# Last product with the mixed tokens stationary, gate and last norm on rows, plain transposes in place of products with a diagonal

## The reference, cut to what matters

```python
def second_block(x, c, ada_w, ada_b, norm_g, w_in, ..., w_out, final_g):
    mod = silu(c) @ ada_w + ada_b                 # 3 x 1024 numbers, one row for all tokens
    shift, scale, gate = split(mod, 3)
    h = rmsnorm(x, norm_g) * (1 + scale) + shift
    p = h @ w_in
    ...                                           # conv branch, RWKV branch
    m = sigmoid(g_conv) * y_conv + sigmoid(g_rwkv) * y_rwkv
    out = m @ w_out                               # the last product, 1024 x 1024
    x = x + gate * out
    return rmsnorm(x, final_g)
# the first block ends: x = x + swiglu(rmsnorm(x, norm_ffn)); x = rmsnorm(x, norm_final)
```

## Time and profile before

| | before |
|---|---|
| median of 3 runs | 1160.0 us (1159.91 to 1161.25) |
| the profiled execution's own time | 1160.27 us |
| its span | 1158.4 us |
| PE busy | 1142.2 us, 99% |
| DVE busy | 483.4 us, 42% |
| ACT busy | 235.6 us, 20% |
| DMA | 161.03 MB, mean 139 GB/s |

### The profile page before, as it was taken

How to read it: one execution, slowest core, us unless ns; L and a number is a source line. 1 busy time by engine, 2 the same in 40 slices (tenths; PEclk the granted TensorE clock), 3 DMA queues, 4 the chain that set the end, 5 groups by cost and what they waited for, 6 DMA issues and landing times.

```text
span 1158.4 us, 20043 instructions
## 1 busy us (share of the span) xinstructions
PE 1142.2 (99%) x8492; PEld 954.2 (82%) x8492; DVE 483.4 (42%) x1248; ACT 235.6 (20%) x617; POOL 80.8 (7%) x119
## 2 busy tenths in 40 slices
PE   9999999999999999999999999999999999999997
PEld 7888888888888587677776878888888888887886
DVE  4252332525332111011011566656667767666332
ACT  3031221203200110001001522313232231324001
POOL 1100000000033100000000021020202202010000
PEclk9999999999999999999999999999999999999999
DMA  8566555540557336443554233223232322151330
GB/s 297 202 238 237 167 204 183 188 162 19 182 147 238 123 130 203 165 152 121 194 203 165 68 97 93 92 93 103 85 107 92 111 74 74 38 219 38 109 109 37
DMA packets 52650, 161.03 MB, mean 139 GB/s; under 512 B 6449, under 2 KB 12497, under 8 KB 52562
## 3 DMA queue, kind: packets, MB, share of 16 engines
q1 hardware_dynamic: 51554, 158.12, 40.3%
q10 hardware_dynamic: 1008, 1.63, 0.4%
HBM read 158.63 MB, written 1.10 MB: 138 GB/s over the span
## 4 chain that ended last, share of the span: by engine, by line
PE 93%; DVE 6%; DMA 1%; ACT 0%; issue 0%; ACTq 0%; DVEq 0%
PE bank L402 40%; PE bank L769 18%; PE bank L611 9%; DVE arena L1863 4%; PE bank L926 3%; PE bank L1098 2%; PE bank L534 2%; PE bank L640 2%; PE bank L913 1%; PE bank L744 1%; PE bank L804 1%; PE bank L617 1%; PE bank L470 1%; PE bank L750 1%; PE bank L782 1%; PE bank L495 1%
## 5 line engine op out<-in xcount | busy, mean ns | idle before, releaser
L402 PE MATMUL bank<-hT,slots 128*128 128x256 f32 x1696 | 373.0, 379 | 1.2 <-DVE arena L1568 0.7
L402 PEld LDWEIGHTS bank<-hT,slots 128*128 128x128 f32 x1696 | 321.0, 190 | 48.3 <-issue 4.7
L769 PE MATMUL bank<-hT,slots 128*128 128x256 f32 x1120 | 254.8, 382 | 1.6 <-ACT arena L1346 1.3
L769 PEld LDWEIGHTS bank<-hT,slots 128*128 128x128 f32 x1120 | 209.7, 190 | 30.7 <-issue 2.4
L1863 DVE SCALAR_TENSOR_TENSOR arena<-padA,par,arena 128x256 f32<-128x256 f32 x232 | 114.8, 559 | 0.0
L611 PE MATMUL bank<-slots,arena 128*128 128x512 f32 x240 | 105.3, 592 | 0.0
L402 PE MATMUL bank<-arena,slots 128*128 128x256 f32 x432 | 93.9, 379 | 0.0
L402 PEld LDWEIGHTS bank<-arena,slots 128*128 128x128 f32 x432 | 82.1, 190 | 11.2
L611 PEld LDWEIGHTS bank<-slots,arena 128*128 128x128 f32 x240 | 45.4, 190 | 51.3 <-issue 50.7
L2186 POOL TENSOR_TENSOR arena<-arena 128x256 f32<-128x256 f32 x40 | 33.7, 865 | 573.7 <-PE bank L744 302.3
L1730 DVE SCALAR_TENSOR_TENSOR arena<-arena,bank 128x256 f32<-128x256 f32 x22 | 9.3, 421 | 121.8 <-ACT arena L1246 121.8
(11 more groups left out here) (326 smaller groups left out, 1209.9 us busy)
## 6 DMA issues: line engine op xcount, KB each, us to landing
slots<-in_w_rwkv SPq DMA_DIRECT2D x72, 512.0 KB, 3.5
slots<-in_w_heads SPq DMA_DIRECT2D x68, 512.0 KB, 3.9
slots<-in_w_gu SPq DMA_DIRECT2D x44, 512.0 KB, 4.2
arena<-in_ada_w SPq DMA_DIRECT2D x24, 512.0 KB, 5.9
slots<-in_w_down SPq DMA_DIRECT2D x22, 512.0 KB, 4.1
slots<-in_w_br SPq DMA_DIRECT2D x32, 256.0 KB, 2.6
slots<-in_w_out SPq DMA_DIRECT2D x16, 512.0 KB, 5.6
slots<-in_w_y SPq DMA_DIRECT2D x16, 512.0 KB, 4.8
```

Source lines behind the costliest of these rows:

```text
L402: end = e.matmul(psum, w[:, k * P:(k + 1) * P], rhs[:, k, :], start=k == 0, stop=k == kt - 1)
L769: end = e.matmul(proj(w, q), slot[w][:, k * P:(k + 1) * P], hT[:, k, :], start=k == 0, stop=k == KT - 1)
```

## The change

The tokens of the second block's residual and of its output stay on the partitions.

- Norm2 and norm4: DVE writes the scaled rows to `xn` in two halves of 512 columns, and PE turns them by plain transposes (`turn_half`, `turn_tokens_of`), four a half. ACT, which takes channel tiles 0 to 3, waits for the first half alone.
- Norm3: its turns on PE, its diagonals, and ACT's 16 copies to `x3T` go. In their place `dve_residual` writes `x` as rows: four instructions of DVE over 512 columns.
- Modulation: for shift and scale (n < 8) two transposes of `adaA` and a sum along the row in place of the product with `ones`; the gate (n = 8 to 11) keeps the product, and DVE adds its bias to a row `gate_row`.
- Two rows that are needed on all partitions (`gate_bias`, `fg_row`) are made by DMA: `par`'s columns to DRAM one number at a time, and back as a broadcast. The constants are issued at trip i = 2, not 3, the two broadcasts at trips 4 and 6.
- Last product: `mT`'s token tile is stationary, the weights are moving, in pieces of 512, 256 and 256 columns for t = 0 and then again for t = 1. DVE does gate, residual, sum of squares and weight on each piece; ACT and DVE scale half a token tile each. The output leaves in four DMAs of 256 KB.

The diff, cut to its core:

```diff
-        def turn_scaled(e, b, src, t, by):
-            for k in range(KT):
-                end = e.matmul(turned(b, k), src[:, t, k * P:(k + 1) * P], by, start=True, stop=True)
+        def turn_half(e, b, t, h):
+            for k in range(4 * h, 4 * h + 4):
+                end = e.transpose(turned(b, k), xn[:, t, k * P:(k + 1) * P], ident)
             return end
+        def turn_tokens_of(e, tag, b, t):
+            for h in range(2):
+                e.wait_ge(*dve.upto(f"{tag}.x{2 * t + h}"))
+                turn_half(e, b, t, h).then_inc(*pe.step(f"{tag}.turn{2 * t + h}"))
...
-            e.matmul(bank[2 * (n % 2)][:, T:2 * T], ones, adaA[:, n * T:(n + 1) * T], start=True, stop=True).then_inc(*pe.step(f"mod.mm{n}"))
+            o = bank[2 * (n % 2)]
+            if n < 8:
+                for j in range(2):
+                    end = e.transpose(o[:, T + j * P:T + (j + 1) * P], adaA[:, (2 * n + j) * P:(2 * n + j + 1) * P], ident)
+            else:
+                end = e.matmul(o[:, T:2 * T], ones, adaA[:, n * T:(n + 1) * T], start=True, stop=True)
+            end.then_inc(*pe.step(f"mod.mm{n}"))
...
-            e.wait_ge(*dve.upto("norm4.diag0"))
-            turn_scaled(e, 4, x2, 0, diag[1]).then_inc(*pe.step("norm4.turn0"))
-            e.wait_ge(*dve.upto("norm3.diag0"))
-            turn_scaled(e, 2, x2, 0, diag[0]).then_inc(*pe.step("norm3.turn0"))
+            turn_tokens_of(e, "norm4", 4, 0)
             down(FF_TILES - 1)
...
+        PIECES = ((6, 4, 0, (2, 0)), (10, 2, 4, (3, 1)), (3, 2, 6, (4, 5)))
...
+            for t in range(TT):
+                for n, (s, tiles, first, b) in enumerate(PIECES):
+                    for k in range(first, first + tiles):
+                        e.wait_ge(*in_slot[OUT_Z[k]].upto(f"wz{k}"))
+                    for q in range(KT):
+                        if t == 0 and n == 0:
+                            e.wait_ge(*dve.upto(f"r{max(q, 3)}"))
+                        end = e.matmul(view3(bank[b[t]][:, 0:tiles * P], P), mT[:, q, tokens(t)], slots[:, s:s + tiles, q * P:(q + 1) * P],
+                                       start=q == 0, stop=q == KT - 1)
+                    end.then_inc(*pe.step(f"z{t}.{n}"))
...
+            for t in range(TT):
+                e.wait_ge(*dve.upto(f"norm5.ms{t}"))
+                e.activation(sums[:, 6 + t:7 + t], sums[:, 3 * t + 2:3 * t + 3], ACT.Sqrt).then_inc(*act.step(f"norm5.sd{t}"))
+                e.wait_ge(*dve.upto(f"norm5.rs{t}"))
+                e.activation(ytok[:, t, 0:512], ytok[:, t, 0:512], ACT.Copy, scale=sums[:, 6 + t:7 + t]).then_inc(*act.step(f"y{t}"))
...
-            e.tensor_scalar(diag[t], ident, sums[:, 6 + t:7 + t], None, ALU.mult).then_inc(*dve.step(f"norm2.diag{t}"))
-            e.wait_ge(*pe.upto(f"norm2.turn{t}"))
+            for h in range(2):
+                c = columns_half(h)
+                e.tensor_scalar(xn[:, t, c], x[:, t, c], sums[:, 6 + t:7 + t], None, ALU.mult).then_inc(*dve.step(f"norm2.x{2 * t + h}"))
+            e.wait_ge(*pe.upto(f"norm2.turn{2 * t + 1}"))
...
+        def dve_residual(e, t):
+            for h in range(2):
+                c = columns_half(h)
+                e.scalar_tensor_tensor(out=x[:, t, c], in0=x2[:, t, c], scalar=sums[:, 20 + t:21 + t], in1=grow[:, c],
+                                       op0=ALU.mult, op1=ALU.mult).then_inc(*dve.step(f"norm3.x{2 * t + h}"))
...
+                for h in range(2):
+                    c = columns_half(h)
+                    e.tensor_scalar(xn[:, t, c], x2[:, t, c], sums[:, 20 + t:21 + t], sums[:, 22 + t:23 + t],
+                                    ALU.mult, ALU.mult).then_inc(*dve.step(f"norm4.x{2 * t + h}"))
+                if t == 0:
+                    dve_residual(e, 0)
+                e.wait_ge(*pe.upto(f"norm4.turn{2 * t + 1}"))
...
+            for t in range(TT):
+                for n, (s, tiles, first, b) in enumerate(PIECES):
+                    c = slice(first * P, (first + tiles) * P)
+                    at = 3 * t + n
+                    e.wait_ge(*pe.upto(f"z{t}.{n}"))
+                    e.scalar_tensor_tensor(out=ytok[:, t, c], in0=bank[b[t]][:, 0:tiles * P], scalar=0.25, in1=gate_row[:, c],
+                                           op0=ALU.mult, op1=ALU.mult).then_inc(*dve.step(f"z{t}.g{n}"))
+                    e.wait_ge(*dve.upto(f"z{t}.g{n}"))
+                    e.tensor_tensor(x[:, t, c], ytok[:, t, c], x[:, t, c], ALU.add).then_inc(*dve.step(f"x3.{at}"))
...
+                    e.tensor_tensor_reduce(out=ytok[:, t, c], in0=x[:, t, c], in1=x[:, t, c], scale=1.0 / D,
+                                           scalar=sums[:, at - 1:at] if n else 1e-6, op0=ALU.mult, op1=ALU.add,
+                                           accum_out=sums[:, at:at + 1]).then_inc(*dve.step(f"norm5.sum{at}" if n < 2 else f"norm5.ms{t}"))
...
+                    e.tensor_tensor(ytok[:, t, c], x[:, t, c], fg_row[:, c], ALU.mult).then_inc(*dve.step(f"y{t}.g{n}"))
+                e.wait_ge(*act.upto(f"norm5.sd{t}"))
+                e.reciprocal(sums[:, 6 + t:7 + t], sums[:, 6 + t:7 + t]).then_inc(*dve.step(f"norm5.rs{t}"))
+                e.wait_ge(*dve.upto(f"norm5.rs{t}"))
+                e.tensor_scalar(ytok[:, t, 512:], ytok[:, t, 512:], sums[:, 6 + t:7 + t], None, ALU.mult).then_inc(*dve.step(f"y{t}"))
...
+            e.dma_start(bass.AP(rows_dram, 0, [[1, P], [P, KT]]), PC("final_g", 0, KT), allow_slow_non_contiguous=True).then_inc(*to_rows.step("final_g"))
+            e.dma_start(bass.AP(rows_dram, D, [[1, P], [P, KT]]), PC("ada_b", 16, KT), allow_slow_non_contiguous=True).then_inc(*to_rows.step("gate_bias"))
...
-                if i == 3:
+                if i == 2:
                     sp_block2_constants(e)
+                if i == 4:
+                    e.wait_ge(*to_rows.upto("gate_bias"))
+                    e.dma_start(gate_bias, bass.AP(rows_dram, D, [[0, P], [1, D]])).then_inc(*in_gate.step("gate_bias"))
+                if i == 6:
+                    e.wait_ge(*pe.upto("mod.mm7"))
+                    e.dma_start(fg_row, bass.AP(rows_dram, 0, [[0, P], [1, D]])).then_inc(*in_fg.step("final_g"))
```

More of the change, by code:

```diff
@@ L191, in build @@
         cum_dram = nc.dram_tensor("cum_scratch", [2 * NH, 3 * P], F32, kind="Internal")
+        rows_dram = nc.dram_tensor("rows_scratch", [2, D], F32, kind="Internal")
         def C(name, n=P, rows=P, off=0):
@@ L279, in build @@
         tg = [carve(T) for _ in range(FF_STEP)]
-        diag = [carve(P) for _ in range(4)]
-        gsq = arena[:, 24 * T:24 * T + D]
+        grow = arena[:, 24 * T:24 * T + D]
+        gsq = arena[:, 28 * T:28 * T + D]
+        gate_bias = arena[:, 0:D]
+        gate_row, fg_row = adaA[:, 0:D], adaA[:, D:2 * D]
         x2 = arena[:, 16 * T:16 * T + TT * D].rearrange("p (t d) -> p t d", t=TT)
-        mod = small[:, 0:24]
+        mod = small[:, 0:16]
         gs = small[:, 24:32]
@@ L1234, in act_norm2 @@
                 e.activation(sums[:, 4 + t:5 + t], sums[:, 4 + t:5 + t], ACT.Sqrt, scale=1.0 / D).then_inc(*act.step(f"norm2.sd{t}"))
-                e.wait_ge(*pe.upto(f"norm2.turn{t}"))
+                e.wait_ge(*pe.upto(f"norm2.turn{2 * t}"))
                 for k in range(4):
@@ L1260, in scaled @@
             def scaled(t):
-                e.wait_ge(*pe.upto(f"norm4.turn{t}"))
+                e.wait_ge(*pe.upto(f"norm4.turn{2 * t}"))
                 for k in range(4):
@@ L1282, in act_norm34 @@
             e.activation(TW[0:HD, :], low[0:HD, :], ACT.Tanh).then_inc(*act.step("TW"))
-        def act_residual(e, t, lo, hi):
-            for k in range(lo, hi):
-                e.activation(x3T[:, k, tokens(t)], turned(2, k), ACT.Copy, scale=PC("norm_final", k)).then_inc(*act.step(f"norm3.h{k}.{t}"))
         def act_low_rank(e, j):
@@ L1779, in dve_norm34 @@
                 e.wait_ge(*dve.upto(f"norm4.rs{t}"))
-                e.tensor_scalar(diag[1 + 2 * t], ident, sums[:, 20 + t:21 + t], sums[:, 22 + t:23 + t],
-                                ALU.mult, ALU.mult).then_inc(*dve.step(f"norm4.diag{t}"))
-                e.tensor_scalar(diag[2 * t], ident, sums[:, 20 + t:21 + t], None, ALU.mult).then_inc(*dve.step(f"norm3.diag{t}"))
-                e.wait_ge(*pe.upto(f"norm4.turn{t}"))
+                for h in range(2):
[5 more added lines that the diff above has]
+                e.wait_ge(*pe.upto(f"norm4.turn{2 * t + 1}"))
                 for k in range(4, KT):
@@ L2106, in dve_out @@
                 e.scalar_tensor_tensor(out=mT[:, m, :], in0=mT[:, m, :], scalar=0.5, in1=m0[m % 2], op0=ALU.mult, op1=ALU.add).then_inc(*dve.step(f"r{m}"))
-            for k in range(KT):
-                e.wait_ge(*pe.upto(f"z{k}"))
-                e.scalar_tensor_tensor(out=x3T[:, k, :], in0=half(k % 3), scalar=mod[:, 16 + k:17 + k], in1=x3T[:, k, :],
-                                       op0=ALU.mult, op1=ALU.add).then_inc(*dve.step(f"z{k}"))
-                e.wait_ge(*dve.upto(f"z{k}"))
-                if k >= 4:
```

(5 more changed lines are left out.)

102 lines of the change are left out of this document (29 added, 73 removed).

## The result

| | after | before, same sittings |
|---|---|---|
| median | 1149.88 us (4 runs: 1149.06, 1149.06, 1150.7, 1151.05) | 1160.06 us (4 runs, 1159.91 to 1161.25) |
| ratio | 0.9911 [0.9894, 0.9928] | |
| profiled execution, its span | 1149.06, 1147.3 us | 1160.27, 1158.4 us |

The kernel is 10.2 us faster, 11.2 by the two profiled executions. The forecast was 15.4, and its range ended at 1148.5.

What follows compares the result with a forecast made beforehand. The prediction took PE, busy 99% of the span, as the bound. Its terms, 1.8 + 1.3 + 6.1 + 6.2 = 15.4 us, gave a median of 1144.6 us, with an 8-in-10 range of 1142.9 to 1148.5.

Steps and rivals of the forecast that it cites:

- Step 5: SwiGLU trips: the two small DMAs take 7 us (3 to 11.5), hidden under 9 us free, so nothing is charged.
- cover: SwiGLU trip 2: 9 us free between the DMA engines being done at 440.2 and PE wanting the weights at 447.6.
- rival (a): SwiGLU: small DMAs stall the weights from 0.07 us a packet on; up to 0.11, 1145 to 1150 us; chance 0.17.
- What bounds the kernel: Whole kernel: PE, busy 99% of the span; a microsecond leaving its sequence leaves the span unless a wait fills it.
- Step 1: Norm2: two turns by plain transposes save 0.9 us each, 1.8 us; DVE's scaling of halves charged nothing.
- Step 2: Modulation: two transposes, 0.22 us, replace 0.43; six of n = 0 to 7 gain, 1.3 us.
- Step 3: Norm3 and norm4: cheaper or removed turns and a shorter wait for copies save 2.7 + 0.9 + 1.8 + 0.7 = 6.1 us.
- Rival (b): Norm3 and norm4's gain is given back, by late DVE or an RWKV part not held by PE: 1147.7 to 1150.7; chance 0.08.
- Step 4: Last product and end: PE's last product takes 27.5 us for 31.6, saving 4.1; with the end's 2.1, 6.2 us.
- End: Behind PE's last product: 2.8 + 0.7 + 2.3 + 0.1 = 5.9 us instead of 8.0, between 4.9 and 6.9.
- middle price: Small DMAs: 0.055 us a packet, the middle of 0.026 and 0.09; 7 us for the two.
- Rival (c): The clock falls because of the change's 48 transposes, 5.3 us, taking as much again: 1150 us; chance 0.02.

Runs made afterwards that it cites:

- e1: Changed kernel without its two small DMAs; the two rows come from the host as rows and are broadcast: 1145.99 us, ratio 0.987.
- e3: Kernel before with only the two small DMAs of single numbers added at trip 3, their output unread: 1161.49 us, ratio 1.001.
- e4: Changed kernel with four small DMAs of single numbers in place of two, the added ones unread: 1159.2 us, ratio 0.9993.
- e5: Changed kernel with the same 8 KB written as 128 packets of 32 bytes a DMA, not 1024, rows in another order: 1145.93 us, ratio 0.9871.
- e6: Changed kernel with five unread matmuls of 256 columns filling PE's wait before trip 2's first product: 1148.83 us, ratio 0.99.
- e10: Changed kernel with the two small DMAs issued behind the first two loads of trip 3: 1147.59 us, ratio 0.9897, one run of 1283.75 left out.
- e7: e1 with norm2's second turn one half product earlier: 1146.74 us, ratio 0.9879 to the kernel before.
- e2: Changed kernel with the group of constants, the two small DMAs in it, back at trip 3 instead of 2: 1149.26 us, ratio 0.9896.

## Why the prediction was wrong

Step 5 failed, which put the small DMAs' wait at nothing. Its cover of 9 us was 6.1, and that is the larger part of the error; its price of 7 us was 8.0. What happened is rival (a) by its outcome, the stalled weights, to which it gave 0.17, but not by its condition: the price stayed below the 0.07 us a packet from which (a) was to begin. Point by point:

- **What bounds the kernel**: right. In e1, where PE's sequence is the whole difference, its savings arrive one for one: 1.8 + 1.3 + 5.8 + 4.1 + 2.1 = 15.1 us of the steps and the 0.2 of the kernel's start are the 15.3 between the spans (1158.4 - 1143.1).
- **Step 1, norm2, 1.8 us**: 1.8 measured. From the start of the first turn to the next product behind the copies it was 411.41 - 392.50 = 18.9 us and is 17.1 (409.26 - 392.17). DVE's scaling of halves delays nothing, and its copies hold PE as before.
- **Step 2, modulation, 1.3 us**: 1.3. 0.22 us for each up to n = 7; a trip takes 21.12 us instead of 21.54.
- **Step 3, norm3 and norm4, 6.1 us**: 5.8 (20.8 to 15.0). No turn waits for DVE. The missing 0.3 is in the low-rank product of t = 1: from its turn to its end it takes 3.4 us (646.96 - 643.54) and not 3.1; it still runs at the pace of the copies, 2.43 us. Rival (b) falls: nothing is given back behind it (from K's product to the last product 463.0 us before and after).
- **Step 4, last product 4.1 us**: 4.1 (27.56 for 31.6). **End 2.1 us**: 2.1 in e1 (1143.1 - 1137.23 = 5.9) and 1.7 in after (6.2); the last 256 KB land 2.3 us behind the start of their issue in both, and the difference of 0.4 lies between that landing and the end of the span (0.4 us in e1, 0.8 in after). The prediction counted the landing from the end of the issue and had 0.1 behind it, so its 5.9 holds as a sum and not in these two terms.
- **Step 5, the rows by DMA, 0 us**: this is the step that failed. It set "7 us for the two" against a cover of 9, so that they came out as hidden. The runs show 8.0 (after) to 8.6 us (e3) for the two, 0.060 to 0.067 a packet with e4, so the middle of the two bounds (0.026 and 0.09) was nearly right. The cover was not: 6.1 us and not 9. In before it was 7.1 already. The prediction took the first load as landed at 460.1, from the end of the engines' busy time, and it landed at 462.0: 1.9 us. In the change PE also comes to it sooner behind the group's first issue, by its own three cheaper modulations (20.9 us for 21.6), and the load landed 0.3 later behind that issue. With the cover of 9 even 8.6 us would have been hidden; with that of 6.1 the predicted 7 would have brought a wait of 0.9.
- The page of the Trainium skill that was weighed there (DMA: Bandwidth & Descriptors, Specifications: read, change and write back below 512 bytes) was taken as twice the middle price, 14 us and a wait of 5. The measured time lies between the two, nearer the 7, and e5, whose packets are below 512 bytes as well, shows that small size by itself isn't the price: here it went by the number of packets.
- **The price of the wait** was also taken too low. The prediction counted a microsecond of wait as one microsecond; the restart (0.26) and the fall of the granted clock behind it (1.7) made 1.94 us into 3.9. Rival (c) had the clock falling for another reason, the transposes; e1 holds all of them and its mean granted clock is 0.999, so (c) falls too.

Added up by the spans of the profiled executions: 15.3 (e1) - 1.94 - 1.95 - 0.4 (the end) gives 11.0, and 1158.4 - 1147.3 is 11.1. In the medians after is 5.3 us above the forecast: 3.9 from e1 to after (1149.88 - 1145.99), and 1.4 that e1's own median lies above it. Of these 1.4, 1.1 is the spread of e1's runs (1144.88 at a mean clock of 0.999, three near 1146.0 at 0.997); clock dips like those at the start of e4, e6 and e10 or in e7 would fit it, but those three runs have no trace, so it stays open.

## What to carry to other kernels

Count the packets of a small DMA, not its bytes: 8 KB written as single numbers pushed the next load of its queue back by 8 us here, and 2.48 MB moved in 16 us in place of 4.61. What pays is the next transfer in the same queue that a busy engine waits for. Where such a DMA can't be avoided, write whole pieces for each partition and let the reader take their order (e5), lay the row out on the host (e1), or issue it where nothing that is wanted soon stands behind it (e10). Read the cover from the landing of the very transfer that is waited for, not from where the DMA engines stop being busy (here 1.9 us earlier), and take off what the change itself speeds up. When a cost is known only between two bounds and its cover lies between them, the wait is a likely outcome, and its price on TensorE includes the clock that may fall behind it.

## What the runs showed of the hardware

- The granted clock can fall behind one short idle stretch in an otherwise full sequence: after 1.94 us of idle, PE worked for 1.4 us at the 2.4 GHz level and then for some 3.4 us at 1.2 GHz, which cost 1.7 us. After waits of 1.5 us in e2 and e3 it stayed at the top in their profiled executions, and only 0.26 us went to the restart; with the wait filled (e6) it stayed as well.
- At the kernel's start, ahead of its first turns, PE waits for DVE, for a time that differs between executions. In e4, e6 and e10 it was 1.98 to 2.04 us, and the clock was at 1.2 GHz between about 12 and 15 us, which cost 1.2 us; in the seven other traces it was 0.87 to 1.76, and the clock stayed.
- The same wait doesn't always bring it. At about 672 us in e1 and e7 every kernel here waits 1.2 us for DVE, works for some 3 us, and waits for ACT. The clock stayed at 1.00 in seven traces and fell in three, between the two waits: for about 3 us in e4 and e5 (4.25 and 4.21 us for the 16 instructions that take 3.69) and for 6 in e7 (6.08). What decides it, no run here shows. Such falls put 0.5 to 2.4 us of spread on single executions of one kernel, more than some of the edits tried here are worth.
- Writes of 4 bytes to DRAM were over in the DMA engines' records within 2 us for 2048 of them, and landed up to 7.8 us behind the last of these records (e10). What stood behind them in the queue was pushed back by 0.060 to 0.067 us for each packet of an engine (after, e3, e4), and its own packets took 1.17 us in place of 0.14 meanwhile. The same bytes in 256 packets of 32 bytes landed within 5.3 us and pushed nothing back that PE waited for (e5).
